# Hybrid decoder step: mask tables made in the projection, and the start of the mixer phase reordered

## Chip, cores and metric

One Trainium2 chip, one of its cores. The metric is device time of the whole kernel in microseconds (us), the median over its runs.

## What is computed

One layer of a hybrid decoder, for a prompt of 2048 tokens and for 8 x 4 new sample tokens. Every array is float32. The core of it:

```python
h = rmsnorm(x, norm_g)
proj = einsum('bld,de->ble', h, w_in)
qkv = causal_short_conv(x_ext, conv_w)
g = -exp(a_log) * softplus(a_in + dt_bias)
o_a, s_new = gated_delta_rule(qa, ka, va, g, sigmoid(b_in), s0)
o_a = rmsnorm(o_a, dn_norm_g) * silu(z_a)
parts = [dilated_branch_prompt(qb, kb, vb, w // d, d) for w, d in ((128, 1), (512, 4), (2048, 16))]
o_b = merge_dilations(parts) * silu(z_b)
y = rmsnorm(x + concat(o_a, o_b) @ w_out, final_norm_g)
```

The delta rule has 4 heads of 128 x 128 and needs, per chunk of tokens, decays exp(gc_i - gc_j) and the inverse of a unit triangular matrix. The window attention has 8 heads of 64, with a causal window of 128 keys and two dilated ones. A query's mask over keys depends only on their distance, so it can be a table.

## The kernel before

The program has four phases, each ended by a barrier of all engines: projection (`project`), mixers (`mixers`), sample tokens, output.

**Projection.** 28 tiles of 128 output channels (7 kinds, q, k, v, za, wq, wk, zb, times 4), each four products of 512 tokens. TensorE does each product three times (high and low parts of the operands). VectorE and ScalarE split, convolve and store. Gates are worked out on VectorE in between; their last step (17 of them) falls into tile 4. `g_row` holds the norm's weights until the rows are normed, and gate scratch after that.

**Mixers, first pass** (line 1746 for VectorE, 1429 for TensorE, 1157 for GpSimd, 1462 for ScalarE, 984 for SP). 16 chunks of 128 tokens. Per chunk: GpSimd multiplies gates into a triangle (`gm`, L1161, two instructions); TensorE makes decay exponents in `pt_ps` and the products of k and q with k in `kq_ps`, from a ring of five buffers that SP fills (L885); ScalarE takes the exp (L1466); VectorE makes `nt` and `attn` (L1544, L1547), two buffers each, which ScalarE's queue stores to DRAM (L1455, L1457); GpSimd masks the diagonal blocks (L1141) and VectorE gathers them (L1554), SP stores them (L977). VectorE may write chunk c only when the stores of chunk c - 2 have landed.

Woven into this pass, before: VectorE's class folds after chunk 1, near table after 2 (L1702 to L1708), class table after 3 and 4 (L1712 to L1723), sample gates after 4 (L1727), scales after 6; GpSimd's iotas at chunk 1, sample masks at 3, block masks at 8, identity blocks at 10; TensorE's sums of gates at 5 (L1423), with exps on ScalarE. From chunk 7 to 14 each chunk also does one of the eight near score units of head 0 (`EARLY`); the ten class units follow the pass (`FIRST_SCORES`), then spread, swap, peak. The score lines (L1623, L1629) add a mask table to the scores.

SP's queue at the start: five ring loads, the six operand loads of head 0 (L858 to L861, 256 KB each, 64 partitions of 8 KB), then `g_dn` (L983, 128 values of 4 bytes). After the last corner store has landed SP issues the gathered corners, the six operand loads of head 1, tokens and kq of chunks 0 and 1, zb (L880), and then the loads of nt and attn.

**The walk.** After that, each engine follows an order that a planner wrote out (`head_order`): the attention of a head, the scores of the next head and two chunks of the delta rule, woven by cost. In head 0's order VectorE first does a substitution of 15 steps (L1565, L1567) on the corners and a flip (L1672). SP stores and reloads the result; GpSimd spreads it (L1189); TensorE's cross products (L1283) follow. VectorE's `score` steps of head 1 come behind the flip. `g_dn` is read by L1611 only.

## Time and profile before

| | us |
|---|---|
| median of 3 runs | 1940.05 |
| lowest, highest | 1934.4, 1942.07 |
| profiled execution | 1935.3 |
| its span, first to last instruction | 1933.6 |
| TensorE busy in the span | 1739.5 (90%) |
| VectorE, ScalarE, GpSimd busy | 835.5, 640.2, 371.9 |
| mean granted TensorE clock | 0.933 |

Times in the rows are counted from the span's start. PE is TensorE, PEld its weight load, DVE VectorE, ACT ScalarE, POOL GpSimd, SPq and ACTq the queues from which SP and ScalarE issue DMAs. L1544 is line 1544 of the kernel before. The projection runs to about 842 us, the mixers from there to about 1500.

### The profile page before, as it was taken

The numbers are of one execution on the slowest core, as the hardware profiler recorded it, in microseconds if no ns is written. First come the engines' busy times: TensorE is split into PE (matmuls) and PEld (weight loads), VectorE is DVE, ScalarE is ACT, GpSimd is POOL, SyncE is SP. The second block draws the span as 40 slices with busy tenths as digits, with TensorE's granted clock in tenths as the row PEclk, the third lists the DMA queues.
The fourth block names the chain that finished last, engine by engine and source line by source line (L and its number), as shares of the span: only waits on it lengthen the run. The fifth ranks groups of instructions, "written<-read, shape, count | busy, mean of one in ns | idle before, by whom it ended". The sixth has DMA issues, their size and how long they took to land. (4 is left out here: it accounts for less than half of the span.)

```text
span 1933.6 us, 27678 instructions
## 1 busy us (share of the span) xinstructions
PE 1739.5 (90%) x9686; PEld 1432.3 (74%) x9686; DVE 835.5 (43%) x1904; ACT 640.2 (33%) x1550; POOL 371.9 (19%) x388
## 2 busy tenths in 40 slices
PE   5999999999999999968788899889899568889897
PEld 5998878888888888846678778778877446667674
DVE  3535312521441253139853453444443464445452
ACT  4524222411331142111424344444345223333332
POOL 0000000000000000037142341341342342432331
PEclk9999999999999999988798898999899568999998
DMA  5425686787468868777856636645430476665660
GB/s 170 131 61 134 139 267 191 144 205 218 109 174 228 212 145 184 216 230 237 235 135 163 163 86 146 170 113 113 120 110 17 142 212 178 192 163 174 163 201 27
DMA packets 227546, 310.10 MB, mean 160 GB/s; under 512 B 62892, under 2 KB 176044, under 8 KB 217948
## 3 DMA queue, kind: packets, MB, share of 16 engines
q1 hardware_dynamic: 222820, 300.15, 58.4%
q10 hardware_dynamic: 4608, 8.39, 1.2%
q8 instruction: 72, 1.18, 0.3%
q14 instruction: 46, 0.38, 0.1%
HBM read 228.50 MB, written 146.97 MB: 194 GB/s over the span
## 5 line engine op out<-in xcount | busy, mean ns | idle before, releaser
L342 PE MATMUL pj<-hT_hi,w_hi 128*128 128x512 f32 x896 | 361.8, 404 | 1.8 <-DVE raw L595 1.8
L343 PE MATMUL pj<-hT_lo,w_hi 128*128 128x512 f32 x896 | 354.6, 396 | 0.0
L344 PE MATMUL pj<-hT_hi,w_lo 128*128 128x512 f32 x896 | 354.3, 395 | 0.0
L344 PEld LDWEIGHTS pj<-hT_hi,w_lo 128*128 128x128 f32 x896 | 168.4, 188 | 40.8
L342 PEld LDWEIGHTS pj<-hT_hi,w_hi 128*128 128x128 f32 x896 | 168.6, 188 | 39.6 <-issue 2.1
L343 PEld LDWEIGHTS pj<-hT_lo,w_hi 128*128 128x128 f32 x896 | 168.8, 188 | 36.8
L1161 POOL TENSOR_TENSOR gm<-upto,g_hi 128x512 fp32r<-128x512 f32 x16 | 16.6, 1040 | 840.3 <-POOLq L2590 839.9
L1412 PE MATMUL o_ps<-pt,vt 128*65 128x256 f32 (+3 forms) x560 | 149.3, 393 | 3.2 <-DVE ot L1679 2.2
L1514 ACT ACTIVATE pt<-pt_ps 128x512 f32<-128x512 f32 x144 | 84.7, 588 | 162.4 <-PE pt_ps L1390 161.9
L2316 PE MATMUL y_bank<-wo_hi,mh 128*128 128x512 f32 (+1 forms) x272 | 113.1, 416 | 6.8 <-POOL ml L2301 4.6
L557 DVE SCALAR_TENSOR_TENSOR acc<-raw,conv_wt,acc 128x512 f32<-128x512 f32 x144 | 108.3, 752 | 5.1
L2317 PE MATMUL y_bank<-wo_lo,mh 128*128 128x512 f32 (+1 forms) x272 | 109.7, 403 | 0.0
L2318 PE MATMUL y_bank<-wo_hi,ml 128*128 128x512 f32 (+1 forms) x272 | 109.6, 403 | 0.0
L1412 PEld LDWEIGHTS o_ps<-pt,vt 128*65 128x65 f32 x560 | 73.8, 143 | 34.6 <-issue 23.2
L546 DVE TENSOR_TENSOR w_lo<-w_raw,w_hi 128x1024 fp32r<-128x1024 f32 x28 | 34.3, 1224 | 116.9 <-ACT w_hi L420 116.7
L652 DVE TENSOR_TENSOR lo<-pj,hi 128x512 fp32r<-128x512 f32 x32 | 22.1, 691 | 143.7 <-ACT hi L515 124.6
L658 DVE COPY xr<-tp 128x512 f32<-128x512 f32 x64 | 43.9, 686 | 80.3 <-PE tp L362 50.9
L503 ACT ACTIVATE sil<-acc 128x512 f32<-128x512 f32 x48 | 30.4, 633 | 140.9 <-DVE acc L557 140.9
L1507 ACT ACTIVATE sc_near<-sc_near,ntop 128x256 f32<-128x256 f32 (+1 forms) x128 | 53.4, 490 | 68.0 <-DVE ntop L1658 68.0
L506 ACT ACTIVATE xr<-pj 128x512 f32<-128x512 f32 x32 | 19.1, 598 | 165.3 <-PE pj L344 105.3
L1629 DVE CUSTOM_DVE_ANT_0 sc_class<-s_ps,class_tab 128x512 f32<-128x512 f32 (+3 forms) x128 | 58.8, 488 | 33.7 <-PE s_ps L1360 23.1
L1293 PE MATMUL d_ps<-tri,cross 128*128 128x64 f32 x384 | 70.4, 288 | 0.0
(460 smaller groups left out, 3585.1 us busy)
## 6 DMA issues: line engine op xcount, KB each, us to landing
out_dram<-in_cache_k_win_dram SPq DMA_DIRECT2D x56, 584.0 KB, 8.2
out_dram<-in_cache_v_win_dram SPq DMA_DIRECT2D x56, 584.0 KB, 8.8
w_raw<-in_w_in_dram SPq DMA_DIRECT2D x31, 512.0 KB, 12.3
kq_all<-sil SPq DMA_DIRECT2D x32, 256.0 KB, 5.2
wqk<-hi SPq DMA_DIRECT2D x32, 256.0 KB, 5.3
wqk<-lo SPq DMA_DIRECT2D x32, 256.0 KB, 5.1
sc_class<-kq_all SPq DMA_DIRECT2D x16, 512.0 KB, 5.1
qs<-wqk SPq DMA_DIRECT2D x16, 512.0 KB, 7.9
```

The source lines that it names most:

```text
L342: pe.matmul(out, w_hi[s][:, k, :], hT_hi[:, k, cols], start=(k == 0), stop=False)
L343: pe.matmul(out, w_hi[s][:, k, :], hT_lo[:, k, cols], start=False, stop=False)
L344: mm = pe.matmul(out, w_lo[s][:, k, :], hT_hi[:, k, cols], start=False, stop=(k == KT - 1))
L557: dve.scalar_tensor_tensor(out=a, in0=x(r), scalar=w(r), in1=a, op0=ALU.mult, op1=ALU.add).then_inc(chain if r < CONV_W - 1 else conv_done, 1)
L1293: mm = pe.matmul(d_ps[u][:, 256 + 64 * n:256 + 64 * n + 64], x[:, n, :], blocks(tt[u], l, 1)[:, n], start=True, stop=True)
L1412: mm = pe.matmul(o_ps[g % 2][0:HD + 1, P * first:P * first + w], vt[:, n, :], pt[:, k % CUTS, at:at + w], start=opened, stop=False, skip_g ...
L1507: ins = act.activation(p, p, ACT.Exp, bias=m)
L1514: act.activation(pt[:, k % CUTS, 0:w], pt_ps[k % 2][:, 0:w], ACT.Copy).then_inc(S["turned_out"], 1)
L1629: ins = dve.tensor_tensor_reduce(sc_class[:, r, class_at(b):class_at(b + 1)], s_ps[k % 2][:, at:at + w], E.class_tab[:, CHUNK - w:], SCALE ...
L2316: pe.matmul(y_ps[0:rows, :], mh[:, u, k, 0:rows], w_hi[:, k, cs], start=(k == 0), stop=False)
L2317: pe.matmul(y_ps[0:rows, :], mh[:, u, k, 0:rows], w_lo[:, k, cs], start=False, stop=False)
L2318: mm = pe.matmul(y_ps[0:rows, :], ml[:, u, k, 0:rows], w_hi[:, k, cs], start=False, stop=(k == KT - 1))
```

## The change

- The two mask tables (near 128 x 256, class 128 x 512) are made in the projection, in halves: the class table at tiles 6 and 13, the near table at tile 20, by VectorE, from iotas of GpSimd that wait for the 17th gate step. Scratch is `g_row`. SP waits for them at tile 21 and stores 393 KB to a DRAM tensor `tables`; at the phase's end it waits for that store. The mixers load it after the five ring loads, and VectorE waits for it before chunk 7.
- The six operand loads of head 0 are issued one per chunk behind the ring load of chunks 0 to 4, the sixth also at chunk 4.
- The load of `g_dn` moves behind the load of zb, after the pass. VectorE's waits for it and for the block masks move behind the first scores, ahead of the walk.
- GpSimd's sample masks, identity and block masks follow the pass; ones and halves are set at chunk 3.
- Sample gates come behind score unit 14, the sums of gates behind the class scores and ahead of the swap, in the banks `d_ps`; ScalarE's six exps behind its last store; VectorE's negation of the decay behind the peak.

Cut to its core:

```diff
@@ -243,6 +249,9 @@
             for t, j, y, kind in TILES:
+                if t == TABLES_AT[2] + 1:
+                    sp.wait_ge(table_done, 3)
+                    sp.dma_start(D.tables, g_row[:, 0:2 * P + CHUNK]).then_inc(tables_out, 16)
@@ -296,6 +306,14 @@
                 pool.affine_select(out=t[:], in_=t[:], compare_op=op, fill=0.0, base=0, pattern=[[step, P]], channel_multiplier=-step).then_inc(tables, 1)
+            pool.wait_ge(gate_step, GATE_STEPS)
+            for x in range(2):
+                if x:
+                    pool.wait_ge(table_done, x)
+                pool.iota(near_tab.bitcast(I32), pattern=[[-1, 2 * P]], base=CHUNK - P - 2 * P * x, channel_multiplier=1).then_inc(iota_done, 1)
+            pool.wait_ge(table_done, 2)
+            pool.iota(row_at, pattern=[[0, 1]], base=0, channel_multiplier=1).then_inc(iota_done, 1)
+            pool.iota(near_tab.bitcast(I32), pattern=[[P, 2], [1, CLASSES], [CLASSES, RUN]], base=-P, channel_multiplier=0).then_inc(iota_done, 1)
@@ -627,6 +645,37 @@
+            worked = 0
+
+            def next_of_table(ins):
+                nonlocal worked
+                worked += 1
+                ins.then_inc(table_step, 1)
+                dve.wait_ge(table_step, worked)
+
+            def class_half(x):
+                step, a, w = near_tab.bitcast(I32), spare, class_tab[:, 2 * P * x:2 * P * x + 2 * P]
+                dve.wait_ge(iota_done, x + 1)
+                next_of_table(dve.tensor_scalar(a.bitcast(I32), step, CLASSES - 1, None, ALU.bitwise_and))
+                next_of_table(dve.tensor_scalar(w, a.bitcast(I32), 0, None, ALU.is_equal))
+                next_of_table(dve.tensor_scalar(a, step, float(P), None, ALU.is_le))
+                next_of_table(dve.tensor_tensor(w, w, a, ALU.add))
+                next_of_table(dve.tensor_scalar(a, step, 0.0, None, ALU.is_ge))
+                next_of_table(dve.tensor_tensor(w, w, a, ALU.mult))
+                next_of_table(dve.tensor_scalar(a, w, 2.0, LN2 / SCALE, ALU.is_ge, ALU.mult))
+                next_of_table(dve.tensor_scalar(near_tab, w, 1.0, NEG, ALU.is_lt, ALU.mult))
+                dve.tensor_tensor(w, a, near_tab, ALU.add).then_inc(table_done, 1)
+
+            def near_half():
+                dve.wait_ge(iota_done, 4)
+                next_of_table(dve.tensor_copy(tok_at, row_at))
+                a, b = spare, near_tab
+                next_of_table(dve.tensor_scalar(a, near_tab.bitcast(I32), tok_at, None, ALU.subtract))
+                next_of_table(dve.tensor_scalar(b, a, 0.0, None, ALU.is_le))
+                next_of_table(dve.tensor_scalar(a, a, float(-P), None, ALU.is_ge))
+                next_of_table(dve.tensor_tensor(a, a, b, ALU.mult))
+                dve.tensor_scalar(near_tab, a, -NEG, NEG, ALU.mult, ALU.add).then_inc(table_done, 1)
+
@@ -636,6 +685,10 @@
                     split(t + 1)
+                if t in TABLES_AT[0:2]:
+                    class_half(TABLES_AT.index(t))
+                elif t in TABLES_AT:
+                    near_half()
@@ -861,6 +915,13 @@
+def load_qk_piece_from(sp, D, env, h, e, x):
+
+    of, half_, part = ((0, 0, 0), (1, 0, 0), (2, 0, 1), (1, 1, 0), (2, 1, 1), (0, 1, 1))[x]
+    to = env.operands[of][e][HD * half_:HD * half_ + HD, :].bitcast(F32)
+    sp.dma_start(to, D.wqk[int(of > 0), part, bass.ds(HD * h, HD), :]).then_inc(env.qk_in[e], 16)
+
+
@@ -978,9 +1038,7 @@
                 load_kq_from(sp, D, E, c, ring[c], ring_in[c])
-            load_qk_from(sp, D, E, 0, 0)
-            with nc.allow_non_contiguous_dma(reason="one column"):
-                sp.dma_start(E.g_dn[:], D.dn_norm_g.unsqueeze(1)).then_inc(g_dn_in, 16)
+            sp.dma_start(E.tables[:], D.tables).then_inc(tables_in, 16)
@@ -989,6 +1047,10 @@
                     load_kq_from(sp, D, env, c + RING, ring[c % RING], ring_in[c % RING])
+                if c < 5:
+                    load_qk_piece_from(sp, D, E, 0, 0, c)
+                if c == 4:
+                    load_qk_piece_from(sp, D, E, 0, 0, 5)
@@ -1000,6 +1062,8 @@
             load_z_from(sp, D, E, 0)
+            with nc.allow_non_contiguous_dma(reason="one column"):
+                sp.dma_start(E.g_dn[:], D.dn_norm_g.unsqueeze(1)).then_inc(g_dn_in, 16)
@@ -1163,22 +1227,17 @@
                     own_blocks()
-                    pool.iota(row_at, pattern=[[0, 1]], base=0, channel_multiplier=1).then_inc(iota_done, 1)
-                    pool.iota(key_at, pattern=[[P, 2], [1, CLASSES], [CLASSES, RUN]], base=-P, channel_multiplier=0).then_inc(iota_done, 1)
-                    pool.iota(step_at, pattern=[[-1, CHUNK]], base=CHUNK - P, channel_multiplier=1).then_inc(iota_done, 1)
                 if c == 3:
-                    sample_masks()
-                if c == 8:
-                    block_masks()
-                if c == 10:
-                    pool.memset(solved, 0.0).then_inc(S["eye_set"], 1)
                     pool.memset(half[:], -0.5).then_inc(S["zeroed"], 1)
-                    pool.wait_ge(S["eye_set"], 1)
-                    for j in range(BASE):
-                        pool.memset(solved[:, j, :, j:j + 1], 1.0).then_inc(S["eye_set"], 1)
                 mask_corners(c)
+            sample_masks()
+            pool.memset(solved, 0.0).then_inc(S["eye_set"], 1)
+            pool.wait_ge(S["eye_set"], 1)
+            for j in range(BASE):
+                pool.memset(solved[:, j, :, j:j + 1], 1.0).then_inc(S["eye_set"], 1)
+            block_masks()
@@ -1417,21 +1476,18 @@
                 pe.wait_ge(S["gb_made"], 1)
+                pe.wait_ge(S["attn_made"], NT)
                 for x, of in enumerate((E.upto, E.ones, E.after)):
-                    pe.matmul(s_ps[0][:, N * x:N * x + N], of[:], gt, start=True, stop=True)
-                pe.matmul(s_ps[1][0:NS, 0:H], E.s_upto[:], gs, start=True, stop=True)
-                pe.matmul(s_ps[1][0:NS, H:2 * H], E.s_after[:], gs, start=True, stop=True)
-                pe.matmul(s_ps[1][:, 2 * H:2 * H + H * DEC_BATCH], E.ones[0:NS, :], gb.rearrange("p h b -> p (h b)"), start=True, stop=True).then_inc(sums_mm, 1)
+                    pe.matmul(d_ps[0][:, N * x:N * x + N], of[:], gt, start=True, stop=True)
+                pe.matmul(d_ps[1][0:NS, 0:H], E.s_upto[:], gs, start=True, stop=True)
+                pe.matmul(d_ps[1][0:NS, H:2 * H], E.s_after[:], gs, start=True, stop=True)
+                pe.matmul(d_ps[1][:, 2 * H:2 * H + H * DEC_BATCH], E.ones[0:NS, :], gb.rearrange("p h b -> p (h b)"), start=True, stop=True).then_inc(sums_mm, 1)
                 prepare(c)
-                if c == 5:
-                    sums_of_gates()
-                if c == min(EARLY):
-                    pe.wait_ge(sums_exped, 6)
@@ -1439,7 +1495,10 @@
                     swap(0)
+                elif step == "spread":
+                    sums_of_gates()
             pe.wait_ge(S["ones_set"], 1)
+            pe.wait_ge(sums_exped, 6)
@@ -1466,16 +1525,15 @@
                     store_chunk(c - 1)
-                if c == 5:
-                    act.wait_ge(sums_mm, 1)
-                    N = NT * H
-                    for x, t in enumerate((E.egc, E.gl, E.dl)):
-                        act.activation(t[:].rearrange("p n h -> p (n h)"), s_ps[0][:, N * x:N * x + N], ACT.Exp).then_inc(sums_exped, 1)
-                    act.activation(E.s_egc[:], s_ps[1][0:NS, 0:H], ACT.Exp).then_inc(sums_exped, 1)
-                    act.activation(E.s_dl[:], s_ps[1][0:NS, H:2 * H], ACT.Exp).then_inc(sums_exped, 1)
-                    act.activation(E.s_gl[:].rearrange("p h b -> p (h b)"), s_ps[1][:, 2 * H:2 * H + H * DEC_BATCH], ACT.Exp).then_inc(sums_exped, 1)
             store_chunk(NT - 1)
+            act.wait_ge(sums_mm, 1)
+            N = NT * H
+            for x, t in enumerate((E.egc, E.gl, E.dl)):
+                act.activation(t[:].rearrange("p n h -> p (n h)"), d_ps[0][:, N * x:N * x + N], ACT.Exp).then_inc(sums_exped, 1)
+            act.activation(E.s_egc[:], d_ps[1][0:NS, 0:H], ACT.Exp).then_inc(sums_exped, 1)
+            act.activation(E.s_dl[:], d_ps[1][0:NS, H:2 * H], ACT.Exp).then_inc(sums_exped, 1)
+            act.activation(E.s_gl[:].rearrange("p h b -> p (h b)"), d_ps[1][:, 2 * H:2 * H + H * DEC_BATCH], ACT.Exp).then_inc(sums_exped, 1)
@@ -1697,31 +1755,6 @@
-            def near_table():
...
-            def class_steps():
...
-            def class_table():
...
@@ -1733,6 +1766,8 @@
                 dve.tensor_scalar(E.rq2[:], E.rq2[:], 1.0 / DK, None, ALU.mult).then_inc(scales_made, 1)
+
+            def negative_decay():
@@ -1749,27 +1784,25 @@
                     class_folds()
-                if c == 2:
-                    near_table()
-                if c == 3:
-                    class_steps()
-                if c == 4:
-                    sample_gates()
-                    class_table()
                     scales()
+                if c == min(EARLY):
+                    dve.wait_ge(tables_in, 16)
             gather_corners(NT - 1)
-            dve.wait_ge(masks_made, 2)
-            dve.wait_ge(g_dn_in, 16)
                     score(0, a[0])
+                    if a[0] == 14:
+                        sample_gates()
                     peak(0)
+            negative_decay()
+            dve.wait_ge(masks_made, 2)
+            dve.wait_ge(g_dn_in, 16)
@@ -2606,6 +2639,7 @@
     D.k_tok, D.v_tok = scratch("k_tok", [SEQ, QK_W]), scratch("v_tok", [SEQ, QK_W])
+    D.tables = scratch("tables", [P, 2 * P + CHUNK])
```

## Rows read from the trace of the kernel before

**Rows 1.** Busy time by stretch: PE, PEld, DVE, ACT, POOL, then PEclk, DMA share, GB/s
```profile
800.00:820.00 20.00, 20.00 (x106) 16.19 (x105) 3.56 (x6) 4.22 (x9) 0.00 (x0) 1.00 0.72 199
...
860.00:863.00 3.00, 0.96 (x3) 0.48 (x3) 0.00 (x0) 0.00 (x0) 0.27 (x1) 0.85 1.06 287
...
881.00:884.00 3.00, 0.00 (x0) 0.00 (x0) 2.97 (x8) 0.00 (x0) 1.43 (x2) 0.77 0.21 80
...
899.00:902.00 3.00, 3.00 (x16) 2.65 (x17) 3.00 (x10) 0.60 (x1) 3.00 (x4) 1.00 0.95 322
...
944.00:947.00 3.00, 1.92 (x7) 1.56 (x8) 2.83 (x6) 2.15 (x6) 0.00 (x0) 0.50 0.95 185
...
950.00:953.00 3.00, 3.00 (x19) 2.37 (x17) 2.93 (x3) 2.70 (x7) 0.00 (x0) 0.86 1.11 377
```

**Rows 2.** Timeline of VectorE: start us, us, instruction [idle before and its releaser]
```profile
857.78 0.23 DVE L1698 COPY fold<-tri 128x128 f32<-128x128 f32 x1
867.63 0.61 DVE L1544 SCALAR_TENSOR_TENSOR d_nt<-d_ps,d,d_oo 128x128 f32<-128x128 f32 x2 [9.63 <-DMA attn_all<-d_attn]
...
870.27 0.14 DVE L1702 CAST tri<-tri 128x1 f32<-128x1 int32 x1
...
873.24 0.29 DVE L1708 TENSOR_SCALAR near_tab<-tri 128x256 f32<-128x256 f32 x1
...
876.20 1.24 DVE L1712 TENSOR_SCALAR tri<-tri 128x512 int32<-128x512 int32 x1
...
880.31 0.69 DVE L1717 TENSOR_TENSOR class_tab<-class_tab,tri 128x512 f32<-128x512 f32 x1
...
883.66 1.00 DVE L1727 TENSOR_TENSOR gb<-gate_g,s_own 32x32 f32<-32x32 f32 x1
...
886.60 0.69 DVE L1723 TENSOR_TENSOR class_tab<-tri 128x512 f32<-128x512 f32 x1
...
895.65 0.61 DVE L1544 SCALAR_TENSOR_TENSOR d_nt<-o_ps,d,d_sg 128x128 f32<-128x128 f32 x2
...
939.86 0.16 DVE L1565 TENSOR_TENSOR tri<-cross 128x4 f32<-128x4 f32 x1
...
959.50 1.06 DVE L1672 COPY cross<-cross 128x1024 f32<-128x1024 f32 x1
```

**Rows 3.** Timeline of SP's queue: when each transfer was issued
```profile
842.25 3.29 SPq L885 DMA_DIRECT2D sc_class<-kq_all  x5
...
848.99 0.60 SPq L861 DMA_DIRECT2D kl<-wqk  x1
849.63 0.59 SPq L983 DMA_DIRECT2D g_dn<-in_dn_norm_g_dram  x1
...
939.14 2.60 SPq L880 DMA_DIRECT2D zb<-zb_ch  x1
```

**Rows 4.** DMA issues (845.4, 848.9, 849.6, 852.3, 938 us): KB each, us to landing
```profile
sc_class<-kq_all SPq DMA_DIRECT2D x1, 512.0 KB, 7.4
...
kl<-wqk SPq DMA_DIRECT2D x1, 512.0 KB, 18.2
...
g_dn<-in_dn_norm_g_dram SPq DMA_DIRECT2D x1, 0.5 KB, 18.0
...
attn_all<-d_attn ACTq DMA_DIRECT2D x1, 256.0 KB, 14.9
...
zb<-zb_ch SPq DMA_DIRECT2D x1, 512.0 KB, 20.0
```

**Rows 5.** Timeline of TensorE: gate sums, and first cross product of the walk
```profile
884.81 0.66 PE L1423 MATMUL s_ps<-gate_g,upto 128*128 128x64 f32 x2 [5.82 <-DVE gb L1727]
...
974.61 1.00 PE L1283 MATMUL d_ps<-tri,d_nt 128*128 128x64 f32 x8
```

**Rows 6.** Timeline of GpSimd: first product of the inverse with its mask
```profile
971.05 1.06 POOL L1189 TENSOR_TENSOR tri<-inv_t,own 128x512 f32<-128x512 f32 x1 [4.24 <-DMA inv_l<-inv_all]
```

**Rows 7.** Costliest groups of the page: busy, mean ns of one | idle before
```profile
L1161 POOL TENSOR_TENSOR gm<-upto,g_hi 128x512 fp32r<-128x512 f32 x16 | 16.6, 1040 | 840.3 <-POOLq L2590 839.9
```

More of the change, by code:

```diff
@@ L132, in project @@
         gx, gy, gz = (g_row[:, 128 * i:128 * i + (NT + 1) * DN_HEADS].rearrange("p (n h) -> p n h", h=DN_HEADS) for i in range(3))
+        near_tab, class_tab, spare = g_row[:, 0:2 * P], g_row[:, 2 * P:2 * P + CHUNK], g_row[:, 2 * P + CHUNK:]
+        row_at, tok_at = stat[:, 0, 0:1].bitcast(I32), stat[:, 0, 1:2]
         at_wv = lambda j: slice(P * j + (AB if j >= 2 else 0), P * j + P + (AB if j >= 2 else 0))
@@ L158, in project @@
         tail_done, tail_stored, raw_head = sem("tail_done"), sem("tail_stored"), sem("raw_head")
+        iota_done, table_step, table_done, tables_out = (sem(n) for n in ("iota_done", "table_step", "table_done", "tables_out"))
         gates_in, gate_step, gate_exps, gate_log, tables = (sem(n) for n in ("gates_in", "gate_step", "gate_exps", "gate_log", "tables"))
         block = ctx.enter_context(nc.Block())
+        GATE_STEPS = 17
+        TABLES_AT = (6, 13, 20)
         TILES = [(NK * j + y, j, y, kind) for j in range(NJ) for y, kind in enumerate(KINDS)]
@@ L274, in _ @@
                         sp.dma_start(D.new_conv[:, P * at:P * at + P].rearrange("r p -> p r"), conv_tail[:, at, :]).then_inc(tail_stored, 16)
+            sp.wait_ge(tables_out, 16)
             sp.wait_ge(tail_stored, 16 * 3 * NJ)
@@ L718, in mixer_tables @@
         sb(n, [P, NT, H]) for n in ("d2", "rinv", "rq", "rq2", "egc", "negc", "dl", "gl"))
-    env.near_tab, env.class_tab = sb("near_tab", [P, 2 * P]), sb("class_tab", [P, CHUNK])
+    env.tables = sb("near_and_class_tab", [P, 2 * P + CHUNK])
+    env.near_tab, env.class_tab = env.tables[:, 0:2 * P], env.tables[:, 2 * P:]
     env.part, env.fold = sb("part", [P, 2, CLASSES]), sb("fold", [P, 2, P])
@@ L940, in mixers @@
             for n in "nt_out attn_out nt_in tt_made tl_made cross_mm cross_made double_mm tl_doubled tt_doubled".split())
-        g_dn_in, root_ready, rooted, mixer_step, tables, iota_done = (sem(n) for n in ("g_dn_in", "root_ready", "rooted", "mixer_step", "m_tables", "iota_done"))
+        g_dn_in, root_ready, rooted, mixer_step, tables, tables_in = (sem(n) for n in ("g_dn_in", "root_ready", "rooted", "mixer_step", "m_tables", "tables_in"))
         masks_made, sums_mm, sums_exped, scales_made = (sem(n) for n in ("masks_made", "sums_mm", "sums_exped", "scales_made"))
         gb = half_gb[:]
-        wa, wb, step_at = flat(tri[:, 0]), flat(tri[:, 1]), flat(tri[:, 2]).bitcast(I32)
-        key_at, row_at, tok_at = tri[:, 3, 0:2].rearrange("p h t -> p (h t)").bitcast(I32), tri[:, 3, 2, 0:1].bitcast(I32), tri[:, 3, 2, 1:2]
+        wa = flat(tri[:, 0])
         corner_out = [sem(f"corner_out{e}") for e in range(2)]
@@ L1698, in class_folds @@
                 then(dve.tensor_copy(E.fold[:, 1].rearrange("p (i r) -> p i r", r=CLASSES), wa[:, 0:RUN].unsqueeze(2).to_broadcast([P, RUN, CLASSES])))
-            def near_table():
-                dve.wait_ge(iota_done, 3)
-                then(dve.tensor_copy(tok_at, row_at))
-                a, b = wa[:, 0:2 * P], wb[:, 0:2 * P]
-                then(dve.tensor_scalar(a, key_at, tok_at, None, ALU.subtract))
-                then(dve.tensor_scalar(b, a, 0.0, None, ALU.is_le))
-                then(dve.tensor_scalar(a, a, float(-P), None, ALU.is_ge))
-                then(dve.tensor_tensor(a, a, b, ALU.mult))
-                then(dve.tensor_scalar(E.near_tab[:], a, -NEG, NEG, ALU.mult, ALU.add))
-            def class_steps():
-                a, w = wa, E.class_tab[:]
-                then(dve.tensor_scalar(a.bitcast(I32), step_at, CLASSES - 1, None, ALU.bitwise_and))
-                then(dve.tensor_scalar(w, a.bitcast(I32), 0, None, ALU.is_equal))
-                then(dve.tensor_scalar(a, step_at, float(P), None, ALU.is_le))
-                then(dve.tensor_tensor(w, w, a, ALU.add))
-                then(dve.tensor_scalar(a, step_at, 0.0, None, ALU.is_ge))
-                then(dve.tensor_tensor(w, w, a, ALU.mult))
-            def class_table():
-                a, b, w = wa, wb, E.class_tab[:]
-                then(dve.tensor_scalar(a, w, 2.0, LN2 / SCALE, ALU.is_ge, ALU.mult))
-                then(dve.tensor_scalar(b, w, 1.0, NEG, ALU.is_lt, ALU.mult))
-                then(dve.tensor_tensor(w, a, b, ALU.add))
             def sample_gates():
```

## The prediction

> **What bounds the kernel now.** I read the whole-kernel page first and then the table of stretches, because the change touches one place only: the start of the mixer phase, from 842 to about 976 us. In the projection TensorE is busy 20.00 of 20.00 us, while VectorE works 3.56, ScalarE 4.22 and GpSimd nothing [rows 1], from 800 to 820. After 842 that stops. From 860 to 863 TensorE works 0.96 us of 3 with the DMA share at 1.06: transfers are the bound. From 881 to 884 TensorE does nothing, VectorE is busy 2.97 of 3 us, DMA 0.21: VectorE is the bound. From 899 to 902 the pass runs at its pace with VectorE and GpSimd both at 3.00 of 3.00 and DMA at 0.95, three resources nearly full at once. That the third is nearly full matters below.
>
> The timeline of VectorE [rows 2] gives the chunks. Chunk 2 starts at 867.63 after 9.63 us of waiting for the store of attn of chunk 0. Chunk 7, the first after the prologue work, starts at 895.65. The near table sits between chunks at 870.27 to about 873.5, the class steps at 876.20 to 881.0, sample gates and the rest of the class table at 883.66 to 887.3: 3.3 + 4.8 + 3.7 = 11.8 us, all on VectorE's path. The pass and the class scores end at 939.86, where the substitution chain of head 0 starts. It ends at 959.50 with the flip. Its result goes out and comes back by DMA, GpSimd spreads it from 971.05, and TensorE takes the first cross product at 974.61 [rows 5, 6]. This chain has little slack: the first pair of GpSimd's products, 1.06 us each, is ready at about 973, when TensorE arrives.
>
> **Part 1, the tables move to the projection.** 9 + 9 + 6 VectorE instructions of 256 columns go to tiles 6, 13 and 20, the slow zb tiles in which VectorE is busy 3.56 of 20 us [rows 1]. The same work costs 11.8 us less the gates now, about 10, so at most 4 to 5 us go into one tile, where every 20 us leave VectorE 16 to spare, beside TensorE's products. I cost it at nothing. If that cover were missing it would be 10 us. GpSimd has four iotas in an idle phase and queues nothing behind its wait for the gates. SP waits for the tables at the head of tile 21, with weight load 23 and that tile's stores behind it. The last table is made at the head of tile 20, a whole tile earlier, so the wait is met. The store is 0.39 MB, about 1.2 us of DMA beside a saturated TensorE. Nothing.
>
> **Part 2, the pass from chunk 2 to 7.** Taking 10 us of tables out does not give 10 us, because DMA comes up as the next bound. The sum of transfers: the five ring loads are issued from 842.25 to 845.5, the fifth takes 7.4 us from then, so it lands at 852.9 [rows 3, 4]. The last of the six operand loads is issued at 848.99 and takes 18.2, landing at 867.2. So six loads take 14.3 us, 2.38 each for 256 KB, while three of the chunk stores (0.79 MB) landed beside them or just after; the first attn store took 14.9 us for it. In steady state a chunk moves one ring load and two stores, 1.05 MB, at 322 GB/s for a share of 0.95 [rows 1], which is 339 GB/s for a full one: 3.1 us. After the change the DMA engines must move, before chunk 7 has its buffers: tables 1.2, six chunks 6 x 3.1 = 18.6, the six operand pieces 14.3, less 2.3 for the stores already counted inside them. 852.9 + 1.2 + 18.6 + 14.3 - 2.3 = 884.7. Chunk 7 starts at 884.7 instead of 895.65: **11.0 us gained**. Spreading the six loads moves bytes in time, it doesn't remove them; the wait of 9.63 us becomes several of 1 to 2 us at chunks 3 to 6.
>
> Bounds: if DMA did not bind, chunk 2 could start at 858.0 (the class folds end there [rows 2]) and five chunks would go at GpSimd's pace of two gm products of 1.04 and one mask product of the same size [rows 7], 3.1 us, with the scales 1.5: chunk 7 at 875.0, 20.6 us gained. If stores get no free ride and TensorE, half idle in that stretch, stays at its lower clock for two chunks more (2 us), chunk 7 starts at 889.0, 6.6 us gained. I take 11.0, by the row of a full DMA share. From chunk 7 to 15 nothing changes: VectorE-bound before and after.
>
> **Part 3, the end of the pass.** Sample gates (two small instructions, 0.4 to 2.0 us: 2.0 at 883.66, where each took 1 us beside GpSimd), the gate sums on TensorE before the swap (884.81 to about 887.1 at the lower clock, 2.3 us [rows 5], half of that hidden in the wait for the spread) and the negation (a copy's 0.2) are now on the way to the substitution: 1 to 4.5 us. GpSimd's sample masks, the identity and the block masks are small instructions that follow its last mask product; ten class scores of VectorE lie between that product and the moment VectorE asks for them. The six exps on ScalarE precede an exp that waits for VectorE anyway. I cost all of it at nothing only because of part 4, which is longer.
>
> **Part 4, the load of g_dn.** This decides. VectorE waits for g_dn before its walk, so before the substitution. The load now stands in SP's queue behind the second head's operands, both chunks' tokens, and zb: 4.7 MB. Its zb load is issued at 939.14 and takes 20.0 us, landing at 959.1 [rows 3, 4]. Is a load of 0.5 KB served in its turn? The one row that can say: g_dn was issued at 849.63 and took 18.0 us, landing at 867.6, 0.4 us behind the last operand load, which landed at 867.2. So it is served in turn, and after the change lands 0.4 behind zb, at 959.5 on the old time axis. SP's tail hangs on the last corner store, so it shifts by the same 11.0 us as the pass. VectorE starts the substitution at 959.5 instead of 939.86, less 11.0: **19.6 us lost**. Queued behind that wait: 15 substitution steps, the flip, and then all scores of head 1. TensorE can run the transposes and mixes of head 0 and two score units ahead, then waits for VectorE's masking. Its two chains, scores and inverse, both shift by 19.6; neither has slack [rows 5, 6].
>
 The trace speaks against it for this load, with 18.0 us for 0.5 KB; it is rival B.
>
> **Part 5, the clock.** After the gap between the scores and the first transposes TensorE's granted clock is 0.50 from 944 to 947, the lower level, 1.2 GHz, and 0.86 in 950 to 953 [rows 1]. A 19 us wait will bring the same. The first 7 to 10 us after it are then TensorE-bound at half pace where they were at full pace: 3.5 us lost (1 if VectorE's scoring sets the pace, 5 if all ten count).
>
> **Sum.** -11.0 + 19.6 + 3.5 = +12.1 us. The profiled execution took 1935.3 us around a span of 1933.6, and becomes 1947.4. It lies 4.75 us under the median of the three runs, 1940.05; on the median the forecast is 1952.
>
> **Rivals.** *A, the pass gains far more.* Stores and loads do not collide, chunk 7 starts near 875: -20.6 + 23.1 = +2.5, 1942.5. For it: DMA share falls to 0.21 in 881 to 884, so there is room. Against: that room is used by the six pieces and by chunks that now come faster. *B, on the other side: g_dn lands early.* Its place is VectorE's wait before the walk; the price falls from 19.6 to 941.8 + 3 - 939.9 = 4.9 us, without the clock loss: -11.0 + 4.9 = -6.1, 1934; with a pass that gains 15 or more it is faster by over 0.5%. It decides as soon as g_dn lands before about 951 on the old axis, where the sum is zero. Against it stands the 18.0 us row. *C, the stall is long but covered*, because the inverse is not needed that early: -11.0 + about 2 for part 3 = -9, 1931. Against: VectorE's head 1 scores are behind the same wait, and the cross product started within 2 us of its data [rows 5, 6]. *D, the pass gains only 6.6 and the clock costs 5*: -6.6 + 24.6 = +18, 1958. *E, the change does not do what it says*, the tables in the projection hold up TensorE after all: +3 to +10 on top of the forecast. Against: VectorE's 3.56 of 20.
>
> **How the numbers follow.** A measurement of this kernel tells about 0.5% (9.7 us) from no change. Forecast with its near neighbours 0.50 (most of it just over the bound, some under), A and cases between 0.20, D with E 0.15, B 0.09, C 0.06. Slower by over 0.5%: 0.40 of the forecast's, 0.15 of D and E, 0.03 of A: 0.58. Faster by over 0.5%: half of B and C, and a little: 0.09. The rest, 0.33, within. The range reaches from just under A (1938, with B and C mostly left out) to just above D (1960).
>
> **What would show it.** In the profile after: no table rows between chunks; chunk 2 at 858 to 862; short DMA waits at chunks 3 to 6; DMA share near 1 from 845 to 885; chunk 7 near 885. Then a wait of VectorE for g_dn of 15 to 18 us right before the first substitution step, and TensorE idle for most of it, with the granted clock at 0.50 after it; the first cross product at about 987 (974.6 + 12). In the projection the same times as before to 1 us. The prediction is wrong if VectorE's wait for g_dn is under 8 us, or if chunk 7 starts before 878 or after 891.

## The result, and the profile after

The changed kernel takes 1948.12 us, median of five runs (1941.95 to 1951.89), beside 1939.62 for the kernel before in five runs of the same job: ratio 1.004, 95% interval 1.002 to 1.0059. The forecast was 1952, in a range of 1938 to 1960. The rise is real, since the interval excludes 1, but at 0.4% it lies just inside the 0.5% that the chances called "no change" (the interval reaches over it): the outcome fell in the band given 0.33, and not in "slower", given 0.58. The profiled execution took 1941.95 us around a span of 1940.3, at a mean granted clock of 0.93. The start of the mixers is 1.67 us later than before (844.25 against 842.58), an offset that arises in the first five projection tiles, before VectorE's first table instruction; it is taken off below where it says "on the old axis", and only there.

Stretches of the changed kernel. Columns: PE, PEld, DVE, ACT, POOL busy, granted clock, DMA share, GB/s.
```profile
801.70:821.70 20.00, 20.00 (x106) 16.19 (x105) 3.63 (x6) 4.22 (x9) 0.00 (x0) 1.00 0.62 201
862.00:865.00 3.00, 0.00 (x0) 0.00 (x0) 1.11 (x4) 0.00 (x0) 0.00 (x0) 0.81 1.01 343
883.00:886.00 3.00, 1.85 (x7) 1.22 (x7) 2.96 (x8) 0.51 (x1) 1.43 (x2) 0.72 1.01 390
...
956.00:971.00 15.00, 0.00 (x0) 0.00 (x0) 14.48 (x16) 0.10 (x1) 0.00 (x0) 0.50 0.01 3
971.00:974.00 3.00, 2.16 (x10) 2.19 (x11) 1.75 (x12) 0.00 (x0) 0.00 (x0) 0.50 0.84 336
974.00:977.00 3.00, 3.00 (x13) 1.76 (x12) 1.19 (x8) 0.20 (x1) 2.70 (x2) 0.58 0.60 137
977.00:980.00 3.00, 3.00 (x25) 2.63 (x25) 1.47 (x8) 0.99 (x2) 0.00 (x0) 1.00 1.25 233
```
The projection is what it was [rows 1]. In 883 to 886, where before DMA had fallen to 0.21, it is full. And a hole has opened: fifteen microseconds in which TensorE does nothing, GpSimd does nothing, DMA is at 0.01 and VectorE alone works. Behind it the granted clock is 0.50, the 1.2 GHz level, in 971 to 974, 0.58 on average in the next 3 us, and 1.00 from 977.

Timeline of VectorE, changed kernel (start us, us, instruction, idle before and its releaser).
```profile
863.89 0.61 DVE L1602 SCALAR_TENSOR_TENSOR d_nt<-d_ps,d,d_oo 128x128 f32<-128x128 f32 x2 [4.56 <-DMA attn_all<-d_attn]
...
870.82 0.61 DVE L1602 SCALAR_TENSOR_TENSOR d_nt<-d_ps,d,d_oo 128x128 f32<-128x128 f32 x2 [1.49 <-DMA attn_all<-d_attn]
...
876.05 0.61 DVE L1602 SCALAR_TENSOR_TENSOR d_nt<-o_ps,d,d_sg 128x128 f32<-128x128 f32 x2 [2.50 <-DMA attn_all<-d_attn]
...
883.04 0.61 DVE L1602 SCALAR_TENSOR_TENSOR d_nt<-d_ps,d,d_oo 128x128 f32<-128x128 f32 x2 [4.27 <-DMA attn_all<-d_attn]
...
887.95 0.61 DVE L1602 SCALAR_TENSOR_TENSOR d_nt<-o_ps,d,d_sg 128x128 f32<-128x128 f32 x2
...
926.75 0.18 DVE L1760 TENSOR_TENSOR gb<-gate_g,s_own 32x32 f32<-32x32 f32 x1
...
932.54 0.36 DVE L1707 TENSOR_TENSOR wide<-s_ps,part 128x64 f32<-128x64 f32 x2 [1.77 <-PE s_ps L1427]
...
933.64 0.19 DVE L1772 TENSOR_SCALAR negc<-egc 128x64 f32<-128x64 f32 x1
950.76 0.17 DVE L1623 TENSOR_TENSOR tri<-cross 128x4 f32<-128x4 f32 x1 [16.93 <-issue]
```
No table rows stand between the chunks [rows 2]. The single wait of 9.63 us at chunk 2 has become 4.56, 1.49, 2.50 and 4.27 at chunks 2, 4, 5 and 6, and chunk 7 starts at 887.95, 886.28 on the old axis: 9.4 us earlier. Then VectorE is ready at 933.83 and issues nothing until 950.76. The 16.93 us carry no releaser in the view ("issue"). The transfers name it: the first line is the load issued at 930.63, the second the one issued at 933.89.
```profile
zb<-zb_ch SPq DMA_DIRECT2D x1, 512.0 KB, 19.8
g_dn<-in_dn_norm_g_dram SPq DMA_DIRECT2D x1, 0.5 KB, 16.7
```
They land at 950.4 and 950.6, and the substitution starts at 950.76. The table of waits shows the rest of the chain.
```profile
POOL cross L1296 <- DMA inv_all<-cross: 48.9, 1, 48.9
...
PE s_ps L1412 <- DVE top L1681: 18.3, 1, 18.3
DVE tri L1623 <- issue: 16.9, 1, 16.9
```
TensorE waits 18.3 us for VectorE's masking of head 1, which stands behind the substitution. The first cross product:
```profile
987.41 1.00 PE L1342 MATMUL d_ps<-tri,d_nt 128*128 128x64 f32 x8
```
It was at 974.61 [rows 5]: +12.8 us. At the end of the heads, which is counted here from TensorE's last `o_ps` product, the shift is +12.0 (1506.3 against 1494.3), at the end of the span +6.7. These shifts are from span start to span start and hold the 1.67 us offset of the mixers' start: on the old axis the first cross product is 11.1 us later.

### The profile page after: what moved, and what is told of

Same layout as the page of the kernel before. It is cut to its first block and busy times, and to the rows that moved or that the text cites. A ratio compares the mean times of both kernels' runs of the same rounds, so it can differ in the third digit from the quotient of the medians.

```text
span 1940.3 us, 27687 instructions
## 1 busy us (share of the span) xinstructions
PE 1739.0 (90%) x9686; PEld 1433.1 (74%) x9686; DVE 834.5 (43%) x1913; ACT 640.7 (33%) x1550; POOL 371.9 (19%) x389
## 5 line engine op out<-in xcount | busy, mean ns | idle before, releaser
L1687 DVE CUSTOM_DVE_ANT_0 sc_class<-s_ps,near_and_class_tab 128x512 f32<-128x512 f32 (+3 forms) x128 | 58.8, 489 | 32.9 <-PE s_ps L1419 21.9
```

The lines of the kernel that those rows point to most:

```text
L1687: ins = dve.tensor_tensor_reduce(sc_class[:, r, class_at(b):class_at(b + 1)], s_ps[k % 2][:, at:at + w], E.class_tab[:, CHUNK - w:], SCALE ...
```

## The experiments

Twelve kernels in three jobs, five rounds each. A ratio is always to the kernel before on the same chip (medians 1939.9, 1945.3 and 1942.4 us in the three jobs). The two columns of time come from each profiled execution, counted from the first VectorE instruction of the mixers, so that the projection's jitter drops out.

| kernel | chunk 7 after | first cross product after | ratio, 95% interval |
|---|---|---|---|
| before | 53.1 | 132.0 | 1 |
| the change | 43.7 | 143.2 | 1.004 [1.002, 1.0059] |
| a1 change, early scalar | 47.0 | 128.6 | 0.9975 [0.9957, 0.9994] |
| a2 change, scalar waited for at its use | 45.6 | 126.3 | 0.9969 [0.9948, 0.999] |
| a3 before, late scalar | 54.1 | 153.4 | 1.0103 [1.008, 1.0127] |
| a4 = a1, loads not spread | 43.7 | 125.5 | 0.9963 [0.9948, 0.9977] |
| b1 = before + tables moved | 44.9 | 130.0 | 0.9975 [0.9949, 1.0002] |
| b2 = a1 + three loads | 55.1 | 135.3 | 1.0 [0.9972, 1.0028] |
| b3 = a4, full-height loads of other rows | 37.6 | 117.6 | 0.9936 [0.9913, 0.996] |
| b4 = before + loads spread | 44.7 | 125.1 | 0.9972 [0.9946, 0.9999] |
| c3 change, scalar on ScalarE's queue | 45.3 | 126.8 | 0.9971 [0.9949, 0.9992] |

c1, c2 and c4 stand with their text below. a2 and c3 leave the change's pass as it is, and reach chunk 7 after 45.6 and 45.3 us beside its 43.7: a chunk 7 read from one trace is good to about 2 us.

**a1.** The load of the scalar goes back ahead of the pass.
```
             sp.dma_start(E.tables[:], D.tables)...
+            sp.dma_start(E.g_dn[:], D.dn_norm_g.unsqueeze(1))...
...
             load_z_from(sp, D, E, 0)
-            sp.dma_start(E.g_dn[:], D.dn_norm_g.unsqueeze(1))...
```

> The changed kernel with one load put back: g_dn is issued ahead of the pass, behind the tables. Theory 1 (the wait for g_dn ahead of the walk costs its 16.9 us, and about 2 us more at the lower TensorE clock after it): 19 us below the changed kernel's 1948, about 1929, which is 0.995 of the kernel before; VectorE's wait before the first substitution is gone. Rival 1 (the stall lies beside other work, the loss comes from the gate sums and sample gates moved to the end of the pass): 1945 to 1948. Rival 2 (only VectorE's 16.9 us count, nothing for the clock): 1931.

Measured 1934.37. One 0.5 KB load, moved, is worth 0.65% (0.9975 against 1.004), about 13 us, and turns the change from a loss into a small gain. The wait is gone and the first cross product is 14.5 us earlier. The gain over before is smaller than expected: its pass started chunk 7 3.3 us later than the change's, of which about 2 are such scatter.

**a2.** The load stays late; VectorE waits for it only where it first uses it.
```
             negative_decay()
             dve.wait_ge(masks_made, 2)
-            dve.wait_ge(g_dn_in, 16)
...
                 elif step == "turn_o":
+                    if isinstance(h, int) and h == 0 and u == 0:
+                        dve.wait_ge(g_dn_in, 16)
```

> The changed kernel, its g_dn load where the change put it, but VectorE waits for it only at its first reader, the gating of chunk 0, some 58 us later. Theory 1 (what costs is the place of the wait, not the load): the same as with the early load, about 1929. Rival 1: 1945 to 1948. Rival 3 (the tiny load slows the transfers queued behind it): 2 to 5 us above the run with the early load.

Measured 1935.2. The load still takes 18.3 us to land, and costs nothing when the wait stands at its use. It was the place of the wait that made the load critical.

**a3.** Before, with only the late load and the wait behind it.
```
-            sp.dma_start(E.g_dn[:], D.dn_norm_g.unsqueeze(1))...
...
             load_z_from(sp, D, E, 0)
+            sp.dma_start(E.g_dn[:], D.dn_norm_g.unsqueeze(1))...
...
+            dve.wait_ge(g_dn_in, 16)
             walk(dve, attend, delta)
```

> The kernel before with this one part of the change alone: g_dn's load behind zb's, and the wait for it ahead of the walk. Theory 1: the walk starts at about 959.5 instead of 939.9, and 2 us go to the clock: 21 us above the kernel before, about 1961. Rival 1 (the stall is covered): 1939 to 1942.

Measured 1959.2, +19.3 us. Here the profile gives the releaser by name:
```profile
960.14 0.17 DVE L1565 TENSOR_TENSOR tri<-cross 128x4 f32<-128x4 f32 x1 [17.93 <-DMA g_dn<-in_dn_norm_g_dram]
```
This is part 4 by itself: 19.6 forecast, the substitution at 960.14 instead of 939.86 (19.7 later from the mixers' start), the first cross product 21.4 us later from the mixers' start. Rivals B and C are excluded.

**a4.** As a1, with all six operand loads of head 0 ahead of the pass.
```
+            load_qk_from(sp, D, E, 0, 0)
             sp.dma_start(E.tables[:], D.tables)...
...
-                if c < 5:
-                    load_qk_piece_from(sp, D, E, 0, 0, c)
-                if c == 4:
-                    load_qk_piece_from(sp, D, E, 0, 0, 5)
```

> The early g_dn version without the spreading: head 0's six operand loads all issued behind the five ring loads, as in the kernel before; tables still made in the projection. Theory 1 (the transfers bound the pass up to chunk 7, so their order hardly matters): chunk 2 waits to about 868, then chunks follow at 3.1 us, chunk 7 at about 885 against 886 with the spreading: 1928 to 1931. Rival 4 (spreading is worth its own 5 us or more, as the first wait fell from 9.6 to 4.6): 1934 to 1937.

Measured 1933.56, the lowest median of the first job. Ahead of chunk 7 VectorE has one wait for a DMA instead of four:
```profile
870.33 0.61 DVE L1599 SCALAR_TENSOR_TENSOR d_nt<-d_ps,d,d_oo 128x128 f32<-128x128 f32 x2 [9.09 <-DMA attn_all<-d_attn]
```
and still reaches chunk 7 after 43.7 us, like the change. Once the tables are out, spreading is worth nothing that these traces can tell: the same bytes have to pass before chunk 7.

**b1 and b4** each add one half to the kernel before: b1 the tables in the projection (masks, sums, gates, scalar and loads at their old places), b4 the spread loads:
```
-            load_qk_from(sp, D, E, 0, 0)
...
             for c in range(NT):
...
+                if c < 5:
+                    load_qk_piece_from(sp, D, E, 0, 0, c)
+                if c == 4:
+                    load_qk_piece_from(sp, D, E, 0, 0, 5)
```

> The kernel before with only the tables moved into the projection (made there, stored, loaded at the start of the head-pair pass); masks, sample gates, sums of gates, the scalar and the six operand loads at their old places. Theory 1: apart from the scalar, what the change moved behind the pass costs nothing and gains little at either place, so this is within 2 us of the version with the early scalar and all loads ahead (1933.6), say 1934; chunk 7 starts 5 to 7 us earlier than before on before's axis, the first cross product 4 to 5 us earlier. Rival 1: the VectorE and TensorE work taken out of the pass is what made the pass shorter; with it back the pass is 2 to 3 us longer and the time is 1936 to 1938. Rival 2: the pile at the end of the pass is what costs; then this is 1930 to 1932.

> The kernel before with only the spreading of head 0's six operand loads over chunks 0 to 4; tables, masks, sums and scalar as before. Theory 1: chunk 2's wait of 9.6 us shrinks to about 4, and VectorE's table work at chunks 2 and 3 (8.8 us) then runs beside the later loads, so chunk 7 starts 4 to 6 us earlier and the time is 1934 to 1936, as good as moving the tables. Rival 2: the loads that come later hold up chunks 4 to 6 by what chunk 2 gained, as in the pair of versions without the tables; then chunk 7 is within 1.5 us and the time 1938 to 1941. Rival 3: the operand loads queued among the ring's delay the chunks' stores and the later ring loads, and the time is 1943 or more.

Measured 0.9975 and 0.9972: either half gains about 5 us, though b1's interval just reaches 1. a4 also has the tables moved and the loads not spread, and stands at 0.9963. The kernels with both halves are a1, a2 and c3, at 0.9975, 0.9969 and 0.9971: the two together gain no more than one. b1 reaches the first cross product 4.5 us after a4 (130.0 against 125.5) but chunk 7 only 1.2 us after it; the rest comes behind chunk 7: a DMA wait of 3.45 us at chunk 10, for one, and 1.4 us between the flip and the cross product, where b1's granted clock was 0.81 in 961 to 964 and 0.63 in 964 to 967. The intervals of b1 and a4 overlap, so whether the masks and sums gained from their move stays open. In b4 chunk 2 waits 1.05 us, and the table work of chunks 2 to 4 now runs while DMA is full:
```profile
858.86 0.61 DVE L1554 SCALAR_TENSOR_TENSOR d_nt<-d_ps,d,d_oo 128x128 f32<-128x128 f32 x2 [1.05 <-DMA attn_all<-d_attn]
...
867.44 1.23 DVE L1722 TENSOR_SCALAR tri<-tri 128x512 int32<-128x512 int32 x1
```
```profile
860.00:863.00 3.00, 2.60 (x9) 2.10 (x10) 2.93 (x7) 0.60 (x1) 2.95 (x4) 0.75 1.00 306
866.00:869.00 3.00, 1.96 (x8) 1.44 (x8) 2.96 (x5) 0.60 (x1) 2.67 (x3) 1.00 1.11 367
861.00:881.00 20.00, 11.36 (x39) 8.96 (x38) 19.45 (x39) 2.41 (x9) 9.70 (x10) 0.68 1.03 285
```
In the kernel before, the near table at 870 to 873.5 still ran beside a full DMA, but from 873 to 890 the share was 0.44 on average:
```profile
873.00:890.00 17.00, 9.27 (x30) 6.92 (x29) 16.59 (x34) 1.81 (x8) 7.43 (x8) 0.68 0.44 156
```
What the kernel before lost was mostly the succession of the two, transfers first and VectorE's tables after. Either edit puts them side by side, and then DMA is the bound.

**b2.** a1 with three more loads of 512 KB at chunks 0 to 2, into the next head's buffers.
```
+                if c < 3:
+                    sp.dma_start(<a 64-partition half of qs[1] or kh[1]>, D.wqk[0, 0, 0:HD, :]).then_inc(more_in, 16)
...
+            sp.wait_ge(more_in, 48)
             load_qk_from(sp, D, E, 1, 1)
```

> The changed kernel with the early scalar, and three more loads of 512 KB (64 rows each) spread over chunks 0 to 2, into buffers of the next head that are free then; the data are not used. Theory 1: from chunk 2 to chunk 7 the pass is bound by the bytes on the DMA engines, about 2.4 us for each such load, so chunk 7 starts 7 us later than in the version without them (by its pass start) and the time is 1941, 4 to 8 us over 1934.4. Rival 2: the waits come from the latency of each load behind its issue and not from the bytes; then the three add less than 2 us at chunk 7 and the time stays within 2 us of 1934.4.

Measured 1.0, 4.9 us over a1. Chunk 7 starts 8.1 us later, 2.7 per load, and the first cross product 6.7 later. The pass to chunk 7 is bound by DMA. The ratios alone would not show it, since the intervals of b2 and a1 overlap; the traces do.

**b3.** a4 with three 128-partition loads in place of the six. Half of their rows come from another place, so that this kernel does not compute the reference and serves as a measurement only.
```
-            load_qk_from(sp, D, E, 0, 0)
+            for t, of in ((qs[0], D.wqk[0, 0, 0:P, :]), (kh[0], D.wqk[1, 0, 0:P, :]), (kl[0], D.wqk[1, 1, 0:P, :])):
+                sp.dma_start(t[:].bitcast(F32), of).then_inc(qk_in[0], 16)
```

> The version with all operand loads ahead of the pass, with the six loads of 64 partitions by 8 KB for head 0 replaced by three of 128 partitions by 8 KB, the same 3.1 MB; the upper halves hold rows of another place, so the scores of head 0 are computed from other numbers. Theory 1: a transfer into 64 partitions moves 512 KB in about 2.4 us, some 220 GB/s, because only half of the partitions take data; one into 128 partitions moves at the ring loads' rate of about 340 GB/s. The three then take about 9.3 us in place of 14.3, chunk 2 starts about 5 us earlier than in that version (its wait 4 us in place of 9), and the time is 1929, at most 1931. Rival 2: the rate follows the size of the descriptors or the source rows and not the count of partitions; then chunk 2 is where it was within 1 us and the time stays at 1933.6.

Measured 0.9936, 5.2 us under a4's ratio, with intervals that overlap. Two windows at the same distance from the mixers' start, first of a4 (start 845.34), then of b3 (start 847.87):
```profile
855.00:858.00 3.00, 3.00 (x16) 2.58 (x15) 2.62 (x7) 0.63 (x2) 3.00 (x4) 1.00 0.99 221
```
```profile
858.00:861.00 3.00, 3.00 (x15) 2.54 (x14) 2.93 (x9) 0.60 (x1) 3.00 (x6) 1.00 1.01 387
```
```profile
867.25 0.61 DVE L1602 SCALAR_TENSOR_TENSOR d_nt<-d_ps,d,d_oo 128x128 f32<-128x128 f32 x2 [3.67 <-DMA attn_all<-d_attn]
```
The last row is b3's chunk 2: a wait of 3.67 us in place of 9.09. With a full share the half-height loads move 221 GB/s, the full-height ones, with the first stores beside them, 387. A busy share of 1.0 is no fixed number of bytes.

b3 also reads distinct rows where a4 reads k's rows twice, and this could be the cause in place of the height. The kernel before answers it. Its q loads read distinct rows, its k loads the same rows twice, and all fill 64 partitions. The transfers issued at 845.58, 846.42, 847.06 and 847.70:
```profile
qs<-wqk SPq DMA_DIRECT2D x1, 512.0 KB, 9.5
qs<-wqk SPq DMA_DIRECT2D x1, 512.0 KB, 11.0
kh<-wqk SPq DMA_DIRECT2D x1, 512.0 KB, 12.8
kl<-wqk SPq DMA_DIRECT2D x1, 512.0 KB, 14.7
```
They land at 855.1, 857.4, 859.9 and 862.4, behind the last ring load at 852.5: about 2.3 to 2.6 us each, the q loads like the k loads. So it is not the reading twice; what is left between the two forms is the 64 partitions and the size of a load, 512 KB against 1 MB.

**c1, c2, c4.** The same idea with the right data: q's two halves in one transfer, k's rows read twice by a stride of zero. c1 is a4 with it, c2 the kernel before with it, c4 is c2 with head 0's three loads issued at chunks 0 to 2.
```
-QK_DMAS, V_DMAS, KQ_DMAS, CHUNK_DMAS = 6, 4, 1, 5
+QK_DMAS, V_DMAS, KQ_DMAS, CHUNK_DMAS = 3, 4, 1, 5
...
+    sp.dma_start(qs[e][:].bitcast(F32), D.wqk[0, 0:2, r, :]).then_inc(env.qk_in[e], 16)
+    for t, part in ((kh, 0), (kl, 1)):
+        sp.dma_start(t[e][:].bitcast(F32), D.wqk[1, part, r, :].unsqueeze(0).to_broadcast([2, HD, SEQ])).then_inc(env.qk_in[e], 16)
```

> The version with the early scalar and all operand loads ahead, with the six operand loads of 64 partitions of every head joined into three of 128 partitions (q's two halves in one, k's halves each from one set of rows read twice); every buffer gets what it had. Theory 1: the rate follows the partitions that a transfer fills, so that this gains as much as the run with other rows did, 5 us over the version with six loads: ratio to before 0.993 to 0.994, chunk 2's wait about 4 us in place of 9.1, chunk 7 some 6 us earlier after the pass start. Rival 2: reading the same rows twice in one transfer is slower than two reads of their own; then the wait is 7 to 9 us and the ratio 0.996 as before. Rival 3: the larger transfers also shorten the head loops; then the end of the mixers moves by more than the pass, over 10 us.

> The kernel before with the operand loads joined into three for every head, still all ahead of the pass, and nothing of the change under study. Theory 1: chunk 2's wait of 9.6 us falls to about 4, VectorE's table work stays in the open, chunk 7 starts about 5.5 us earlier than before and the time is 0.996 to 0.998 of before, as good as either half of the change alone. Rival 2: the wait is hidden again by a later one; chunk 7 within 1.5 us and ratio 0.999 to 1.001.

> The kernel before with the operand loads joined into three, and head 0's three issued at chunks 0, 1 and 2 in place of ahead of the pass; tables, masks, sums and scalar as before. Theory 1: the bytes on the DMA engines up to chunk 6 take 5 us less than with six loads, and VectorE's table work runs beside them, so it gains over the spread alone (0.9972) until VectorE bounds the pass: ratio 0.994 to 0.996, no chunk wait over 2 us before chunk 7. Rival 2: with the loads spread, VectorE's own work with the tables is already what bounds the pass, and the time stays at 0.997.

All expectations missed by far: 2116.6, 2124.5 and 2121.5 us, ratios 1.0889, 1.0916 and 1.0909. In c1 the stretch after the other transfers have drained:
```profile
880.00:890.00 10.00, 0.00 (x0) 0.00 (x0) 0.00 (x0) 0.00 (x0) 0.00 (x0) 0.50 0.13 54
```
Nothing works but DMA, at a share of 0.13, as much as two of its sixteen engines, with 54 GB/s. For a full share that would be 415 GB/s, which is the pace of b3's loads or better, so the few engines at work are not slow. SP's queue shows what is then stuck:
```profile
847.32 23.01 SPq L913 DMA_DIRECT2D kl<-wqk  x1
870.37 5.82 SPq L1040 DMA_DIRECT2D near_and_class_tab<-tables  x1
876.24 20.30 SPq L1042 DMA_DIRECT2D g_dn<-in_dn_norm_g_dram  x1
```
Issuing took 23.01 us where it takes 0.6, and chunk 4 starts at 925.03 instead of a4's 878.08. By the share, a source of [2, 64 rows, 8 KB] went to two engines, perhaps split along its outer dimension of 2. No kernel was run with the same view in another order, so this cause is argued and not shown.

**c3.** The change, with the scalar's load issued by ScalarE.
```
             store_chunk(NT - 1)
+            act.dma_start(E.g_dn[:], D.dn_norm_g.unsqueeze(1)).then_inc(g_dn_in, 16)
             act.wait_ge(sums_mm, 1)
```

> The changed kernel with the load of the output norm's scalar issued by ScalarE behind its last two stores, in place of SP behind zb. Theory 1: what kept the scalar's 0.5 KB back for 16.7 us is what SP had queued ahead of it (the next heads' operands, tokens and zb), so on ScalarE's queue it lands within 5 us of its issue, VectorE's wait of 16.9 us goes, and the time is that of the version with the early scalar, 0.997 to 0.998 of before. Rival 2: the backlog is in the DMA engines that both queues share; then it lands 12 to 17 us after its issue, VectorE waits 5 to 10 us, and the ratio is 1.000 to 1.002.

Measured 0.9971, and VectorE no longer waits. The load, issued at 921.04:
```profile
g_dn<-in_dn_norm_g_dram ACTq DMA_DIRECT2D x1, 0.5 KB, 2.2
```
Theory 1 gave the number, but the run doesn't prove its cause: SP's operand loads were issued from 924.24 on, so the load had landed, at 923.2, before there was a backlog. It was in front of the bytes in time. That the second queue would have passed a backlog is not shown; the first attn store, on ScalarE's queue too, took 14.9 us beside SP's backlog [rows 4], which speaks against it.

## Why the prediction was right, and where it was not

- **Part 1, tables in the projection: 0 forecast, 0 found.** VectorE 3.63 us of 20, TensorE 20.00; the offset of 1.67 us is there before the first table, and from the sixth tile on every tile takes the same time to 0.02 us in all fourteen traces, with tables and without. Rival E falls. Only the fifth tile varies, 24.1 to 25.8 us in the five traces without tables and 24.4 to 28.9 in the nine with them (24.5 in the change's own, 25.1 before); whether GpSimd's first iota, ahead of it, has a part in that is open.
- **Part 2, the pass: 11.0 forecast, 9.4 measured** at chunk 7, and 7.5 and 7.8 in a2 and c3, which have the same pass. The mechanism held (DMA at 1.01 in 883 to 886; b2 pays 2.7 us a load, forecast 2.38). Chunk 2 came at 862.2 on the old axis, and the waits at chunks 2, 4, 5 and 6 were 1.5 to 4.6 us, longer than the 1 to 2 forecast. One fact was wrong: the prediction and the description of the kernel give an operand load 256 KB. It is 512 KB, as the profile's list of DMA issues and [rows 4] say, so the queue ahead of the scalar held 6.3 MB and not 4.7. The sum is untouched, because it used the measured 2.38 us a load; the correct size means 220 GB/s, which the 221 GB/s of a4's window confirms. "A full share is 339 GB/s" holds for the stretch of ring loads and stores that it was read from, and not for these loads.
- **"Spreading moves bytes in time, it doesn't remove them"** was right beside the moved tables (a4), and incomplete: alone (b4) spreading gains as much as moving the tables.
- **Part 3** came as costed: gates 0.33 us with GpSimd idle, the wait for the swap 1.77 instead of 1.21, negation 0.19, all ahead of the 16.93 us stall.
- **Part 4: substitution 8.6 us later forecast (-11.0 + 19.6), 9.2 measured** on the old axis; the scalar landed 0.2 us behind zb (forecast 0.4). a3 alone gives +19.3. The wait itself was 16.9 us and not 19.6, because VectorE came to it only 7.7 us earlier (932.2 on the old axis against 939.9). That cost nothing more: the start of the substitution hangs on the landing, and SP had issued zb 10.2 us earlier (929.0 on the old axis against 939.14), close to the forecast 11.0.
- **The sentence of the Trainium skill** (DMA: Bandwidth & Descriptors, Queues, rings and completion order), "not FIFO per issuing engine", is no promise that a small load overtakes: the same section of the Trainium skill says that each DMA engine takes its descriptors in ring order. The traces agree: 18.0, 16.7 and 16.0 us (a3) for 0.5 KB say that the load took its turn, and no run here shows it overtaking what one queue had ahead of it.
- **Part 5, the clock: 3.5 forecast, 2.2 measured** (+12.8 at the cross product, +10.6 at the flip). TensorE resumed at 971.84 and had its full clock by 977: about 5 us of half pace, where 7 to 10 were assumed. From the flip to the cross product it took 15.1 us in the four traces before, a1, b4 and c3, at a granted clock of 1.00, and 17.3 here, 17.1 in a3 and 17.0 in b1, where the clock fell to between 0.50 and 0.63 for a part. a2, without such a hole, took 16.3 with a granted clock of 0.72 in its last 4.6 us. So this time goes with the granted clock, hole or no hole.
- **The sum: +12.1 on the profile forecast, +6.7 measured; +8.5 on medians.** The first cross product came at +12.8 (987.41, forecast 987) and the heads ended at +12.0. That it hit 987 so closely is luck: 1.67 us of it is the projection's offset, which the forecast did not have; without it the shift is 11.1. The missing 5.3 us lie in the output phase, whose code the change doesn't touch. From the heads' end to the end of the span it took 439.3 us before and 434.0 after, and 435.7 to 442.9 in the other traces. The granted clock differs there. The same hundred microseconds, the second of the phase, first before, then after:
```profile
1594.30:1694.30 100.00, 85.58 (x405) 63.51 (x404) 45.66 (x90) 36.07 (x60) 33.95 (x20) 0.91 0.65 181
```
```profile
1606.30:1706.30 100.00, 88.59 (x435) 66.58 (x434) 50.67 (x105) 38.34 (x65) 35.50 (x21) 0.97 0.62 177
```
  Why the clock was 0.97 in the one and 0.91 in the other is not known. The forecast had no term for it, and both profiled executions lie below their medians. The measured median came within the range because the mechanism up to the heads' end held; the 4 us that it lies under the forecast are not accounted for term by term.
- **The chances.** A forecast of +12 against a bound of 9.7 was too near it for 0.58 on "slower".

Among the kernels that compute the whole reference a4 has the lowest ratio, 0.9963, and b4 gets 0.9972 with one small edit; their intervals overlap. Both beat the kernel before and the change, by less than the 0.5% bound over the former.

## What to carry to other kernels

Before moving a load, look at two places: what its queue has issued just ahead of it, and where its consumer waits; 0.5 KB behind 6 MB cost 19.3 us at a wait far ahead of its use, and nothing at the use. When a pass shows a DMA wait and then engine work in the open, hide either under the other; here doing both gained once. And after any rewrite of a transfer's shape read the DMA share and the GB/s together.

## What was not expected of the hardware

- A full DMA share is 221 GB/s with 64-partition loads of 8 KB rows and 387 with 128-partition ones and stores; chunk 2's wait shrank by 5.4 us, from 9.09 to 3.67, for the same 3.1 MB of operands.
- A source of two outer blocks of 64 rows left a share of 0.13 and 54 GB/s, and cost 9% of the kernel; two of SP's issue instructions then took 23.0 and 20.3 us.
- Shifts at the first cross product don't all arrive. b3 was 9.1 us early there in its trace (965.48 against 974.61) and 3.3 at the heads' end; a2 was 4.0 early and then 3.5 late. From the first cross product to the heads' end, before and then a2:
```profile
974.61:1494.34 519.73, 478.90 (x3216) 422.52 (x3215) 229.67 (x741) 225.32 (x579) 168.20 (x185) 0.92 0.47 121
```
```profile
970.59:1497.80 527.21, 484.66 (x3216) 427.57 (x3215) 230.38 (x741) 225.50 (x579) 168.71 (x186) 0.91 0.47 119
```
  Of a2's 7.5 us more, 5.8 are TensorE's own busy time for the same number of matmuls, at a granted clock of 0.91 for 0.92; in b3 it is 3.6 (482.5 us at 0.91) of 5.8. Most of what is lost in the heads is thus lost at TensorE's clock. What lowered it was not settled.
